# Attention by groups with the keys' low halves against the queries' high halves alone, in two 64-row matmuls

## The reference, cut to what matters

```python
s = jnp.einsum('bgrqd,bgqnkd->bgrqnk', qi, kg) * scale      # selected blocks: n_top = 8 of 8 blocks
s = jnp.einsum('bqgrd,bkgd->bgrqk', qi, kk) * scale          # window of 512 of 512 tokens
o = o_c * gates[..., 0:1] + o_s * gates[..., 1:2] + o_w * gates[..., 2:3]
```

## Time and profile before

| | |
|---|---|
| median of three runs | 1525.07 us |
| profiled execution | 1524.09 us |
| its span | 1522.3 us |
| TensorE busy | 1468.9 us, 96% of the span |
| VectorE, ScalarE, GpSimd busy | 718.9, 716.8, 677.4 us |
| granted TensorE clock, mean | 0.991 of full speed |
| group stage | about 766 to 1048 us |

### The profile page before, as it was taken

How to read it: one execution, slowest core, us unless ns; L and a number is a source line. 1 busy time by engine, 2 the same in 40 slices (tenths; PEclk the granted TensorE clock), 3 DMA queues, 4 the chain that set the end, 5 groups by cost and what they waited for, 6 DMA issues and landing times.

```text
span 1522.3 us, 23455 instructions
## 1 busy us (share of the span) xinstructions
PE 1468.9 (96%) x7566; PEld 1221.6 (80%) x7566; DVE 718.9 (47%) x1256; ACT 716.8 (47%) x1305; POOL 677.4 (44%) x970
## 2 busy tenths in 40 slices
PE   6999978999999999999999999999999999999998
PEld 5877757888888888877978787878888888888886
DVE  5477772643434300246466767674644444410053
ACT  5245543654444423357365656464744444423262
POOL 4634434365656555364420202111465656555452
PEclk9999998999999999999999999999999999999999
DMA  5321111223232333242510101010132222332221
GB/s 201 121 70 56 55 42 56 94 100 106 87 106 87 106 102 97 70 135 84 167 44 15 56 1 55 14 41 21 66 136 96 96 96 96 96 97 98 97 97 56
DMA packets 37131, 126.22 MB, mean 83 GB/s; under 512 B 6096, under 2 KB 6864, under 8 KB 36816
## 3 DMA queue, kind: packets, MB, share of 16 engines
q1 hardware_dynamic: 31824, 115.88, 22.9%
q10 hardware_dynamic: 5248, 9.55, 1.8%
HBM read 123.32 MB, written 2.10 MB: 82 GB/s over the span
## 4 chain that ended last, share of the span: by engine, by line
PE 58%; issue 17%; POOL 16%; DVE 5%; ACT 4%; POOLq 0%; ACTq 0%; DVEq 0%
PE banks_a L1204 22%; POOL w_lo L297 15%; PE banks_b L1213 9%; PE banks_a L1213 8%; PE banks_a L1576 4%; PE banks_b L1204 4%; PE banks_a L1181 4%; PE banks_b L1548 2%; PE banks_b L1368 2%; DVE nm L940 1%; PE banks_a L1387 1%; PE banks_a L1467 1%; ACT w_hi L358 1%; ACT y L361 1%; PE banks_b L1551 0%
## 5 line engine op out<-in xcount | busy, mean ns | idle before, releaser
L297 POOL TENSOR_TENSOR w_lo<-w_raw,w_hi 128x256 fp32r<-128x256 f32 x852 | 648.0, 793 | 767.0 <-ACT w_hi L358 766.9
L358 ACT ACTIVATE w_hi<-w_raw 128x1024 fp32r<-128x1024 f32 x213 | 225.6, 1061 | 284.1 <-PE banks_b L1213 137.5
L1204 PE MATMUL banks_a<-nT_hi,w_hi 128*128 128x512 f32 (+1 forms) x968 | 344.5, 377 | 0.0
L1204 PE MATMUL banks_a<-nT_lo,w_hi 128*128 128x512 f32 (+1 forms) x968 | 342.7, 375 | 0.0
L1204 PE MATMUL banks_a<-nT_hi,w_lo 128*128 128x512 f32 (+1 forms) x968 | 342.2, 375 | 0.0
L1204 PEld LDWEIGHTS banks_a<-nT_hi,w_hi 128*128 128x128 f32 x968 | 174.6, 190 | 32.0
L1204 PEld LDWEIGHTS banks_a<-nT_hi,w_lo 128*128 128x128 f32 x968 | 173.7, 189 | 32.1
L1204 PEld LDWEIGHTS banks_a<-nT_lo,w_hi 128*128 128x128 f32 x968 | 173.8, 189 | 31.3
L846 DVE SCALAR_TENSOR_TENSOR y<-banks_a,conv,y 128x511 f32<-128x511 f32 x88 | 66.0, 750 | 218.2 <-ACT y L459 217.6
L459 ACT ACTIVATE y<-banks_a,conv 128x512 f32<-128x512 f32 x88 | 68.6, 780 | 207.6 <-PE banks_a L1204 207.5
L940 DVE TENSOR_REDUCE nm<-banks_b 128x2 f32<-128x256 f32 (+2 forms) x96 | 79.2, 825 | 27.1 <-PE banks_b L1371 14.5
(11 more groups left out here) (256 smaller groups left out, 2400.6 us busy)
## 6 DMA issues: line engine op xcount, KB each, us to landing
w_raw<-in_w SPq DMA_DIRECT2D x213, 512.0 KB, 3.3
g_pre<-in_gains ACTq DMA_DIRECT2D x6, 512.0 KB, 5.1
x<-in_x SPq DMA_DIRECT2D x4, 512.0 KB, 9.6
g_post<-in_gains ACTq DMA_DIRECT2D x4, 512.0 KB, 7.6
out<-x SPq DMA_DIRECT2D x4, 512.0 KB, 2.6
pe_raw<-in_pT ACTq DMA_DIRECT2D x2, 512.0 KB, 6.0
w1k<-in_w ACTq DMA_DIRECT2D x1, 1024.0 KB, 4.9
w1v<-in_w ACTq DMA_DIRECT2D x1, 1024.0 KB, 6.9
```

Source lines behind the costliest of these rows:

```text
L297: pool.tensor_tensor(w_lo[slot][:, cols], w_raw[k % RAW][:, cols], w_hi[slot][:, cols].bitcast(F32), ALU.subtract).then_inc(S["w_lo_done"], 1)
L358: act.activation(w_hi[u % RING][:, :], w_raw[u % RAW][:, :], ACT.Copy).then_inc(S["w_hi_done"], 1)
L1204: m = pe.matmul(bank[:, cols], w[:, k * P:(k + 1) * P], r[:, k, cols], start=(k, pas) == (0, 0), stop=(k, pas) == (KT - 1, 2))
```

## The change

Kl has one plane instead of two: rows `side(c)` hold the low part of branch c, and its copy into the other half is gone. A new tile Qx holds, for each head, a copy of the query's high part in the half of the rows where Q[h] has the low part; ScalarE makes these four copies per group after its third weight copy and ahead of its wait for the rotated keys. `gscores` issues the two matmuls with Kh first and then, for each branch, one with 64 rows: the query's high part (Q[h] or Qx, whichever has it in `side(c)`) with Kl. Low x low is no longer computed. TensorE's wait for the low parts and Qx moves behind the first two matmuls with Kh. vT moves into a part of y0 to make room.

```diff
--- before.py
+++ after.py
@@ -199,15 +199,16 @@
             ("w2", [P, 2, HEAD], F32), ("cbias", [P, 2], F32), ("gT", [P, SEQ], F32),
             ("ksh", [HEAD, SEQ], F32), ("kt1", [HEAD, SEQ], F32))
 
-        (_, _, _, _, _, _, _, cm, Vg, vT, Kh, Kl, Q0, Q1, Q2, Q3, gp, gpT, sc, pc, pcT,
+        (_, _, _, _, _, _, _, cm, Vg, Kh, Kl, Q0, Q1, Q2, Q3, Qx, gp, gpT, sc, pc, pcT,
          og) = overlay(
             ("room_group", *room[1:]), *[("again_" + n, s, d) for n, s, d in keep1],
             ("cm", [P, 2, TT * N_PAD], F32),
-            ("Vg", [P, TT, P + HEAD], F32), ("vT", [P, SEQ], F32),
-
-            ("Kh", [P, 2, SEQ], F32R), ("Kl", [P, 2, SEQ], F32R),
+            ("Vg", [P, TT, P + HEAD], F32),
+
+            ("Kh", [P, 2, SEQ], F32R), ("Kl", [P, SEQ], F32R),
 
             ("Q0", [P, SEQ], F32R), ("Q1", [P, SEQ], F32R), ("Q2", [P, SEQ], F32R), ("Q3", [P, SEQ], F32R),
+            ("Qx", [P, 2, SEQ], F32R),
             ("gp", [P, 2, 2, SEQ], F32), ("gpT", [P, 2, 2, SEQ], F32),
             ("sc", [P, TT, GHEADS, N_PAD], F32), ("pc", [P, TT, GHEADS, N_PAD], F32),
             ("pcT", [P, TT, P], F32),
@@ -215,7 +216,7 @@
         Q = [Q0, Q1, Q2, Q3]
 
         gsh, gt1 = xn[:, 0:SEQ], xn[:, SEQ:2 * SEQ]
-        opair = y0
+        opair, vT = y0, y0[:, 2, :]
         oc = y0[:, 2:4, :].rearrange("p a n -> p (a n)").rearrange("p (t h n) -> p t h n", t=TT, h=GHEADS)
         banks_a = ctx.enter_context(nc.psum_tensor("banks_a", [P, 4, 512], F32))
         banks_b = ctx.enter_context(nc.psum_tensor("banks_b", [P, 4, 512], F32))
@@ -231,7 +232,7 @@
         aff_done gateconv_done conv_done gelu_done h_done hhi_done hlo_done
         ple_in pehi_done pelo_done sig_done xhalf_done
         cmpw_in kr_done shifted_done gsig_done gatesT_done hid_done gelc_done kv_done kvc_done kchi_done kclo_done pad_ready cm_in
-        groupkv_done ghi_done glo_done gkx_done vT_done vTt_done vg_done
+        groupkv_done ghi_done glo_done gqx_done vT_done vTt_done vg_done
         csc_done cexp_in cexp_done cp_done cpT_done cpTc_done coc_done oc_done
         gscores_done gnegmax_done gprobs_done gT_done gpTa_done gpTv_done gpv_done
         oread_done opair_done goT_done goThi_done goTlo_done
@@ -719,22 +720,22 @@
                 query_high(1)
                 w_high(u + 2, i, per)
 
+                for h in range(GHEADS):
+                    m = h % 2
+                    signal(act.activation(Qx[side(1 - m), h // 2, :], Q[h][side(m), :].bitcast(F32), ACT.Copy),
+                           "gqx_done", 4 * g + h + 1)
                 act.wait_ge(S["groupkv_done"], 3 * g + 3)
                 for c in range(2):
                     signal(act.activation(Kh[side(c), c, :], B[2][side(c), :], ACT.Copy), "ghi_done", 8 * g + 4 + c + 1)
                 for c in range(2):
                     signal(act.activation(Kh[side(1 - c), c, :], Kh[side(c), c, :].bitcast(F32), ACT.Copy), "ghi_done",
                            8 * g + 6 + c + 1)
-                act.wait_ge(S["glo_done"], 6 * g + 6)
-                for c in range(2):
-                    signal(act.activation(Kl[side(1 - c), c, :], Kl[side(c), c, :].bitcast(F32), ACT.Copy), "gkx_done",
-                           2 * g + c + 1)
                 act.wait_ge(S["cexp_in"], g + 1)
                 signal(act.activation(pc[:, :, :, :], sc[:, :, :, :], ACT.Exp), "cexp_done", g + 1)
                 seq = [(h, k) for h in range(GHEADS) for k in range(TT)]
                 gexps(*seq[0])
                 act.wait_ge(S["units_done"], PLAN["group"] + 4 * g + 4)
-                signal(act.activation(vT[:, :], A[2], ACT.Copy), "vT_done", g + 1)
+                signal(act.activation(vT, A[2], ACT.Copy), "vT_done", g + 1)
                 act.wait_ge(S["cpT_done"], g + 1)
                 signal(act.activation(pcT[:, :, :], A[3].rearrange("p (t n) -> p t n", t=TT), ACT.Copy),
                        "cpTc_done", g + 1)
@@ -1103,7 +1104,7 @@
 
                 for c in range(2):
                     dve.wait_ge(S["ghi_done"], 8 * g + 4 + c + 1)
-                    dve.tensor_tensor(Kl[side(c), c, :], B[2][side(c), :], Kh[side(c), c, :].bitcast(F32),
+                    dve.tensor_tensor(Kl[side(c), :], B[2][side(c), :], Kh[side(c), c, :].bitcast(F32),
                                       ALU.subtract).then_inc(S["glo_done"], 1)
 
                 dve.wait_ge(S["csc_done"], g + 1)
@@ -1539,14 +1540,18 @@
                     n = (qt + 1) * P
                     if (h, k) == (0, 0):
                         pe.wait_ge(S["ghi_done"], 8 * g + 8)
-                        pe.wait_ge(S["gkx_done"], 2 * g + 2)
                     elif (h, k) != (0, 1):
                         pe.wait_ge(S["gprobs_done"], 2 * step(h, k) - 2)
                     for c in range(2):
 
-                        for K in (Kh, Kl):
-                            pe.matmul(B[2 * (k % 2) + c][:, 0:n], Q[h][:, tok(qt)], K[:, c, 0:n],
-                                      start=K is Kh, stop=False)
+                        pe.matmul(B[2 * (k % 2) + c][:, 0:n], Q[h][:, tok(qt)], Kh[:, c, 0:n], start=True, stop=False)
+                    if (h, k) == (0, 0):
+                        pe.wait_ge(S["glo_done"], 6 * g + 6)
+                        pe.wait_ge(S["gqx_done"], 4 * g + 4)
+                    for c in range(2):
+
+                        high = (Q[h][side(c), tok(qt)], Qx[side(c), h // 2, tok(qt)])[c != h % 2]
+                        pe.matmul(B[2 * (k % 2) + c][:, 0:n], high, Kl[side(c), 0:n], start=False, stop=False)
                     for c in range(2):
                         pe.matmul(B[2 * (k % 2) + c][:, n - P:n], ident_b[:, :], causal_b[:, :], start=False,
                                   stop=True).then_inc(S["gscores_done"], 1)
```

## The result

The changed kernel takes 1529.05 us, the median of 8 runs (1528.03 to 1530.9), the one before 1524.62 (8 runs); the ratio is 1.0035, with an interval of 1.0025 to 1.0046. So it is slower by 0.35%, 5.3 us by the ratio. Forecast were 1530.7 us and 0.37%.

The account below looks back on a forecast made before the run. TensorE's order bounds the heads and VectorE's chain each group's start. Copies +3.0 and scores +2.7 make 5.7 us on the profiled 1524.09, 1529.8; with the runs' median 1.0 higher, 1530.7 us, range 1526.5 to 1534.5.

Parts of the forecast that it names:

- Part 1, the copies: Group starts: four Qx copies overrun ScalarE's wait, delaying Kh and VectorE's chain; dropping Kl copies gains nothing; +3.0 us.
- Part 2, the scores: TensorE's score matmuls: the saved stream never pays for switching to half rows and back; +0.67 us per group, +2.7 in all.
- The switch: TensorE going into half rows and back: 0.09 in, 0.11 open load, 0.10 back, 0.01 second half; 0.31 us per step.
- the 128-wide step: Scores of the query tile 128 keys wide: +0.08 us each, two per group on the path.
- the 256-wide step: Scores of the query tile 256 keys wide: +0.16 us, vanishing in TensorE's wait before the eight transposes in all 16 heads.
- (a): Scores: the switch is free, saving 6.2 us less 3.0 at the starts; 1521.9 us, chance 0.12.
- (b): Group starts: the copies cost nothing, leaving +2.7 us alone; 1527.8 us, chance 0.15.
- (c): Scores: the two half-row matmuls do not overlap, one more stream, 5.5 us in all; 1536.2 us, chance 0.07.

Follow-up runs that it names:

- the copies moved up: The changed kernel with its four Qx copies issued two behind each pair of Q copies, in ScalarE's other waits; ratio 1.0015 to the kernel before.
- the second trip: The changed kernel with each step as Kh, half-row Kl, Kh, half-row Kl, so two switches into half rows; ratio 1.0177 to the kernel before.
- one Kl left out: The kernel before without branch 1's Kl matmul, leaving three full-array score matmuls per step and no switch; ratio 0.9982 to the kernel before.
- the run in the same half: The changed kernel with both 64-row matmuls in rows 0 to 63, so they cannot run at once; ratio 1.0082 to the kernel before.

## Why the prediction was right, point by point

**Part 1, the copies**: +3.0 us forecast. Measured 0.95 us at the start of groups two to four and 0.45 in the first, 3.3 us, in the changed kernel; taken away again by moving the copies (start back at 12.28) and put into the kernel before (with the projection moved, 13.25). The term was short by 0.1 us in three groups: between the end of the last copy (851.82) and Kh pass another 0.1 us that I had not counted. That the dropped Kl copies would bring nothing was right; TensorE's wait fell by 0.43 us and the transposes did not gain by it.

**Part 2, the scores**: +2.7 us forecast. The switch came out as read from layer 0: 0.09 us in, 0.11 for the open load, 0.10 back. The term that was mis-sized is the 128-wide step: +0.08 forecast, +0.13 measured. I let the switch begin when the second Kh's stream ends (0.053 us), but from Kh to the pair are 0.21 us, that is the full pace of 0.11 and 0.09. The same shift, smaller, made the others 0.07, 0.10 and 0.17 instead of 0.05, 0.09 and 0.16. A steady head has 0.10 + 0.13 + 0.07 = 0.30 us on the path, and is longer by 0.30; the 256-wide step's 0.17 vanish in the former wait, as forecast. Per group the switches cost 0.74 us with the copies moved up, and 0.7 to 0.9 in the changed kernel (its growth per group less the start's), forecast 0.67. That this is so near is partly luck: four 384-wide, three 512-wide and two 128-wide steps at their measured growths make 0.87. Of the last head's 0.10 only 0.03 come through with the copies moved up, and between the eight transposes of the first head and of the second 0.12 instead of 0.17. So the price was set too low and the count of what lies on the path too high, and the two errors partly cancel.

**The sum**: the starts' 3.3 us and four groups of 0.8 on average make the group stage's 6.45; forecast were 5.7, and the ratio says 5.3 (3.8 to 7.0).

**Rivals.** (a), no price for the switch: refuted by the changed kernel's own blocks, which grew, and by the second trip. The run with one Kl left out says more: even without the price the change would have got about 3 us from TensorE, not the 6.2 that I gave this rival, less 3.3 for the copies: no gain at all. The Trainium skill (TensorE: Matmul & The Clock Gate, Part 3) gives the span of packed matmuls as one matmul's time and some 4 ns per further tile; here the second tile does start within 10 ns, but a pair between full-array matmuls costs 0.3 us more than its stream. The Trainium skill (TensorEngine Tiling (Array Packing), Tiling Modes) says that a change of tiling mode drains TensorE; the holes of 0.09 and 0.10 us at the two changes agree with it. (b), copies for nothing: refuted by both runs on the copies. (c), no overlap: refuted by the run in the same half.

## What to carry to other kernels

Two 64-row matmuls at once save one stream, at most 0.21 us here, and the trip into half rows and back with one load in the open costs 0.3; so gather many half-row matmuls between two switches (no run here tried that), or leave it. Even on an engine that is 98% busy, added work counts only beyond the waits that it fills (here 0.30 of 0.47 us per head), and work taken away only up to the next chain (0.27 of 0.64 us), so price a saving and a cost separately. Put side copies where the engine that makes them idles for long, not in front of the one copy for which the longest chain waits.

## What the runs showed of the hardware

A wait of TensorE can cost more than itself. With a wait of 2.66 us at a group's start the granted clock stood at 0.50 (1.2 of 2.4 GHz) for 3.4 us after it, in groups two to four alike, 1.5 us each; with waits of 1.69, 1.26 and 0.86 us at the same place it stayed at 1.00 in the second, third and fourth group. The length of the wait alone does not decide: after 2.04 us at the first group's start of that same run the clock stayed at 1.00, and after the idle 1.77 us ahead of the compression it fell in eight profiled executions and not in the other five. What else decides stays open. The loss from a longer wait is not proportional to it, and part of the spread between executions of one kernel goes with the granted clock, as the times above show.
